# Gathering the heavy group's rows after the first expert's gate product instead of before it

## The reference

```python
def grouped_moe(h, router_w, router_bias, w_gate, w_up, w_down):
    ...
    g = jnp.argmax(group_score, axis=-1)          # each token picks 1 of 4 groups
    ...                                           # and 2 of the 4 experts in it
    for e in range(N_EXPERTS):                    # 16 experts
        a = jax.nn.silu(hf @ w_gate[e]) * (hf @ w_up[e])
        y = y + combine[:, e:e + 1] * (a @ w_down[e])
```

## Time and profile before

| what | value |
|---|---|
| time, median of 3 runs | 2551.22 us (2542.8 to 2553.99) |
| time of the profiled execution | 2548.41 us |
| its span, first to last instruction | 2546.6 us |
| mean granted TensorE clock | 0.987 of full speed |
| busy: TensorE, VectorE, ScalarE | 2426.7, 1694.0, 1304.5 us |
| mean DMA rate over the span | 212 GB/s |
| first mixture (first and last group of instructions looked at) | about 205 to 520 us |
| second mixture | about 755 to 1110 us |

### The profile page before, as it was taken

How to read it: one execution, slowest core, us unless ns; L and a number is a source line. 1 busy time by engine, 2 the same in 40 slices (tenths; PEclk the granted TensorE clock), 3 DMA queues, 4 the chain that set the end, 5 groups by cost and what they waited for, 6 DMA issues and landing times.

```text
span 2546.6 us, 31351 instructions
## 1 busy us (share of the span) xinstructions
PE 2426.7 (95%) x12650; PEld 2057.4 (81%) x12650; DVE 1694.0 (67%) x1521; ACT 1304.5 (51%) x1795; POOL 93.4 (4%) x121
## 2 busy tenths in 40 slices
PE   4989999999899999999999999899997999999999
PEld 3878888887788888879878888788886888987887
DVE  5767988887769787857455565565557655645654
ACT  2555777434547666634445445454455544444443
POOL 1000000111000000000000001000010000000000
PEclk8999999999999999999999999999999999999999
DMA  8815999984519897945535775155551555553553
GB/s 303 289 34 185 368 368 356 358 308 168 217 39 327 301 331 276 365 160 174 195 128 176 190 273 182 61 175 194 193 180 52 184 195 190 174 198 132 177 188 116
DMA packets 229568, 539.80 MB, mean 212 GB/s; under 512 B 20880, under 2 KB 27568, under 8 KB 229424
## 3 DMA queue, kind: packets, MB, share of 16 engines
q1 hardware_dynamic: 207264, 471.82, 53.1%
q0 software_dynamic: 15520, 59.77, 6.4%
q10 hardware_dynamic: 6640, 6.20, 1.3%
HBM read 533.54 MB, written 4.19 MB: 211 GB/s over the span
## 4 chain that ended last, share of the span: by engine, by line
PE 83%; DVE 10%; ACT 3%; issue 2%; DMA 1%; POOL 1%; ACTq 0%; DVEq 0%
PE pair L1041 7%; PE Y L1206 6%; PE Y L1204 6%; PE Y L1215 6%; PE pair L1469 5%; PE pair L1470 5%; PE pair L1475 5%; PE pair L1084 4%; PE pair L1077 4%; PE pair L1078 4%; PE pair L1050 4%; PE Y L1514 3%; PE Y L1516 3%; PE Y L1524 3%; PE pair L1010 2%; PE pair L1019 2%
## 5 line engine op out<-in xcount | busy, mean ns | idle before, releaser
L2316 DVE TENSOR_TENSOR w_low<-raw,w_high 128x2048 fp32r<-128x2048 f32 (+2 forms) x450 | 1016.0, 2273 | 438.8 <-ACT w_high L1858 437.4
L1858 ACT ACTIVATE w_high<-raw 128x1024 fp32r<-128x1024 f32 (+1 forms) x900 | 896.4, 1049 | 554.1 <-PE pair L1470 169.3
L1077 PE MATMUL pair<-w_high,hT 128*128 128x512 f32 (+1 forms) x596 | 233.1, 392 | 1.6 <-ACT work L1913 0.8
L1078 PE MATMUL pair<-w_high,hT 128*128 128x512 f32 (+1 forms) x596 | 231.9, 390 | 0.0
L1206 PE MATMUL Y<-w_high,gated_low 128*128 128x512 f32 x528 | 205.9, 390 | 0.0
L1204 PE MATMUL Y<-w_high,gated_high 128*128 128x512 f32 x528 | 205.9, 390 | 0.0
L1041 PE MATMUL pair<-hT,w_high 128*128 128x512 f32 x768 | 183.0, 390 | 0.5 <-DVE work L2762 0.5
L1041 PEld LDWEIGHTS pair<-hT,w_high 128*128 128x128 f32 x768 | 142.6, 188 | 29.7 <-DVE work L2762 0.9
L1469 PE MATMUL pair<-w_high,rounded 128*128 128x512 f32 x384 | 154.8, 403 | 0.8 <-DVE gated_low L2660 0.8
L1470 PE MATMUL pair<-w_high,rounded 128*128 128x512 f32 x384 | 152.2, 396 | 0.0
L1084 PE MATMUL pair<-w_low,hT 128*128 128x512 f32 (+1 forms) x596 | 146.8, 388 | 4.0 <-DVE w_low L2316 4.0
(11 more groups left out here) (395 smaller groups left out, 3984.3 us busy)
## 6 DMA issues: line engine op xcount, KB each, us to landing
raw<-in_exp_w_gate SPq DMA_DIRECT2D x128, 512.0 KB, 4.6
raw<-in_exp_w_up SPq DMA_DIRECT2D x128, 512.0 KB, 4.8
raw<-in_exp_w_down SPq DMA_DIRECT2D x128, 512.0 KB, 4.6
raw<-in_w_up SPq DMA_DIRECT2D x128, 512.0 KB, 4.6
raw<-in_w_down SPq DMA_DIRECT2D x128, 512.0 KB, 4.3
raw<-in_ret_w_in SPq DMA_DIRECT2D x96, 512.0 KB, 4.7
work<-in_w_mod POOLq DMA_DIRECT2D x40, 1024.0 KB, 8.1
raw<-in_ret_w_out SPq DMA_DIRECT2D x32, 512.0 KB, 4.0
```

The lines of the kernel that those rows point to most:

```text
L1077: nc.tensor.matmul(ps[:, b, 0:n], in_high[:, k0 + kk, bs], high[:, k, :], start=(kk == 0), stop=False)
L1078: last = nc.tensor.matmul(ps[:, b, 0:n], in_low[:, k0 + kk, bs], high[:, k, :], start=False, stop=False)
L1858: nc.scalar.activation(w_high[:, s % HIGH, part], raw[:, s % RAW, part], ACT.Copy).then_inc(high_ready, 1)
L2316: V.tensor_tensor(w_low[:, s % RAW, 0:n], part, w_high[:, s % HIGH, 0:n].bitcast(F32), ALU.subtract).then_inc(low_ready, 1)
```

## The change

The 32 matmuls that gather the heavy windows leave `gather_tokens` for a function of their own, which TensorE calls for the first expert between the second half of the gate product and the first half of the up product. ScalarE's eight heavy copies move from before the first expert's `feed(g + 4)` to behind its `gate_acts`. The instructions, their shapes and their semaphores are the same. VectorE, SyncE and GpSimd have the same programs.

```diff
+            def gather_heavy(m):
+
+                for k in range(KD):
+                    ps, ks = Y[:, k * S:(k + 1) * S], slice(k * P, (k + 1) * P)
+                    for b in range(TB):
+                        nc.tensor.matmul(ps, xn_high[:, b, ks], sel[:, b, SLOTS:], start=(b == 0), stop=False)
+                        last = nc.tensor.matmul(ps, xn_low[:, b, ks], sel[:, b, SLOTS:],
+                                                start=False, stop=(b == TB - 1))
+                last.then_inc(heavy_gathered, 1)
+
             def gather_tokens(m):
...
                     light(j, xn_low, False).then_inc(fill_done, 1)
-                for k in range(KD):
-                    ps, ks = Y[:, k * S:(k + 1) * S], slice(k * P, (k + 1) * P)
-                    for b in range(TB):
-                        nc.tensor.matmul(ps, xn_high[:, b, ks], sel[:, b, SLOTS:], start=(b == 0), stop=False)
-                        last = nc.tensor.matmul(ps, xn_low[:, b, ks], sel[:, b, SLOTS:],
-                                                start=False, stop=(b == TB - 1))
-                last.then_inc(heavy_gathered, 1)
                 use = m.places
...
                     elif at and not follows_heavy:
                         turn(earlier)
+                    if at == 0:
+                        gather_heavy(m)
                     up_free(units)
...
-                se.wait_ge(heavy_gathered, m.nth + 1)
-                for j in range(2):
-                    for i in range(4):
-                        k = 4 * j + i
-                        last = modulated_copy(heavy_tmp[:, j, i, :], Y[:, k * S:(k + 1) * S], k)
-                    last.then_inc(tmp_made, 1)
+
+                def heavy_copies():
+                    se.wait_ge(heavy_gathered, m.nth + 1)
+                    for j in range(2):
+                        for i in range(4):
+                            k = 4 * j + i
+                            last = modulated_copy(heavy_tmp[:, j, i, :], Y[:, k * S:(k + 1) * S], k)
+                        last.then_inc(tmp_made, 1)
...
                     gate_acts(units, g + 1)
+                    if at == 0:
+                        heavy_copies()
```

## The result

| | before | after |
|---|---|---|
| median of 20 runs each | 2551.26 us | 2560.15 us |
| lowest to highest | 2542.8 to 2559.09 | 2550.89 to 2564.38 |
| profiled execution, its span, its clock | 2548.41, 2546.6, 0.987 | 2564.38, 2562.6, 0.984 |

The ratio is 1.0024, with an interval of 1.0013 to 1.0036. So the change costs 0.0024 x 2551 = 6.1 us (3.3 to 9.2), and the kernel is within 0.5% of before, on the slow side. The forecast was +5.7 us. The difference of the two medians, 8.9 us, is larger than the ratio says but inside its interval. I go by the ratio, since it comes with an interval.

A forecast was written before the change was run, and what follows sets the result against it. TensorE, carrying 83% of the chain, was taken to bound the kernel; 2.85 us in the second mixture plus 2.9 in the first gave 5.7 us slower, forecast 2555.5 us, range 2547 to 2562.

The forecast's parts named there:

- the likeliest case: The whole time stays within 0.5% (12.8 us) of the kernel before; chance 0.88, against slower 0.08 and faster 0.04.
- A: Rival, chance 0.08: transfers bound the mixtures and the change is faster, 2.7 us won, 2548.5 us from the median.
- B: Rival, chance 0.12: TensorE's early waits are real, but a later stretch of TensorE absorbs the delay; 2551 us.
- C: Rival, chance 0.15: VectorE's backlog passes in full to TensorE, or the clock falls in both mixtures; 7.8 to 9.5 us.
- Steps 1 and 2: Start of the mixture: TensorE idles 1.4 us before the places, 0.3 before the first gate half, which starts 2.15 early.
- Step 3: Second gate half waits 0.4 us for VectorE's fourth split, starting at 784.8 instead of 786.54, 1.7 us won.
- The working for the first mixture: First mixture with a clock fall of 1.7 us: first down product 2.9 us late; without the fall 1.2 us.
- Steps 5 and 6: Behind the late copies ScalarE's piece 5 starts 3.9 us late; VectorE's 12.0 us to `gated_low` end at 809.4.
- Steps 4 and 7: First up half 2.15 us late, then 0.7 us idle at the first down product: 2.85 us in the second mixture.
- The clock: The granted clock falls to its lower level in the first mixture, 1.7 us lost, and not in the second.

The follow-up runs named there:

- before, again: The kernel before, unchanged, run once more for its profile; from first light gather matmul to first down product 38.21 us (first mixture, clock fell) and 36.69 us (second).
- the filled kernel: The changed kernel with 6 small matmuls put in TensorE's wait before the places; ratio to the kernel before 1.0008 (0.9992 to 1.0024), median 2555.22 us.
- before, more bytes: The kernel before with a 64 KB memory-to-memory DMA added behind each expert piece, 6% more bytes; one run, 2561.06 us.

## Why the prediction was right

The time after, 2560.15 us, is in the range, within 0.5% of before as the likeliest case had it, and the cost of 6.1 us stands beside a forecast of 5.7. The range alone says little, as it holds the times of all three rivals too. The interval of the cost, 3.3 to 9.2 us, rules out A and B but not C. So the forecast stands or falls with its steps.

- *Steps 1 and 2, the places and the first gate half.* Right: 1.07 us idle and some 0.3 us to restart, then 0.17; alone +1.3. From the first light matmul to the first gate matmul, 13.77 us became 11.61, that is 2.16 early, where 2.15 was forecast. In the second mixture it was 12.42, for a reason that the forecast didn't have (below).
- *Step 3, the second gate half.* Right where the clock stayed up: 0.27 us on the matmul and 0.7 on its weight load, and the first up half came 788.00 - 766.36 - 19.46 = 2.18 us late, where 2.15 was forecast (19.46 is 789.34 - 769.88). Where the clock fell, the first half took so long that the split was there in time. This is why a fall costs 1.55 us before and only 0.9 to 1.2 after. The working for the first mixture is wrong here: it puts the 1.7 us of the fall behind the wait for the split, which makes TensorE 2.15 us late at the up half, and it was 1.65 (22.65 us behind the first light matmul against 21.00).
- *Steps 5 and 6.* Right: 3.9 us of waiting for piece 5 on VectorE without a fall, and 12.0 us from there to `gated_low`. With a fall VectorE waits 4.8 to 5.1, and up to 6.1 with a long one.
- *Steps 4 and 7, the sum per mixture.* 0.65 us idle at the down product against 0.7; in all 3.0 us without a fall against 2.85. With a fall in both kernels it is 40.63 to 40.89 less 38.24, or 2.4 to 2.7, against 2.9.
- *The clock.* The forecast took the first mixture with a fall and the second without, as in the one trace it had. The change has it in both, once for 6.9 us behind a late piece. The mean of the four segments of the change is 41.2, of the four of before 37.5: 3.7 us per mixture, 7.5 in all. If the falls came as often in both kernels it would be 5 to 6, from 2.5 to 3.0 per mixture. The measured 6.1 (3.3 to 9.2) holds both, so the size of the clock's part stays open. The mean granted clock of the timed runs doesn't settle it either: 0.9853 over the 20 runs after and 0.9843 to 0.9849 over the runs before, while one more fall in a mixture is worth only 0.0007.

**What the forecast left out.** It gives no price to a piece that lands late. In the second mixture of the change two halves of the second gate piece did, and the first two lines are ScalarE's there. The other two are ScalarE's in the first mixture of "before, again".

```profile
786.52 1.06 ACT L1863 ACTIVATE w_high<-raw 128x1024 fp32r<-128x1024 f32 x1 [0.37 <-DMA raw<-in_exp_w_gate]
...
787.78 1.06 ACT L1863 ACTIVATE w_high<-raw 128x1024 fp32r<-128x1024 f32 x1 [0.21 <-DMA raw<-in_exp_w_gate]
```

```profile
233.51 1.06 ACT L1858 ACTIVATE w_high<-raw 128x1024 fp32r<-128x1024 f32 x1 [0.19 <-DMA raw<-in_exp_w_gate]
234.79 1.06 ACT L1858 ACTIVATE w_high<-raw 128x1024 fp32r<-128x1024 f32 x1 [0.21 <-DMA raw<-in_exp_w_gate]
```

So the late landing doesn't need the change. But in the kernel before the gather covers it: its gate product began 13.75 us behind the first light matmul all the same. After the change ScalarE's copy of the fourth light step, which stands behind that piece, is what TensorE waits for, 0.98 us instead of 0.17, and the gate product began at 12.42. The same happened once more, in the filled kernel's second run (waits of 0.48 and 0.20 us, gate product at 12.50, 42.66 us). These are the only two mixtures with a long fall, so 0.8 to 0.9 us of their 42.6 is a cost of the change that only shows when a piece is late; whether the late piece also made the fall long isn't shown.

**The rivals.** A (the transfers bound it) fell: nothing got faster, and the row of 403 GB/s shows room in the kernel before. The Trainium skill, DMA: Bandwidth & Descriptors, section "Where 436 GB/s comes from", has the HBM side bind at about 358 GB/s; the traces here disagree, with one core working: 366 over an expert and 403 with bytes added. B (absorbed later) fell: in the second mixture the transposes behind the first down product (L1495, L1498) stand at 817.64 before and 831.32 after, 13.68 later, and the last ones at 1117.57 and 1131.22, 13.65 later. In 300 us nothing of the shift was absorbed. C was half right. VectorE's delay isn't passed on in full, as TensorE is late too by then, but its other condition, a fall in both mixtures, held in every profile of the change. The forecast was right at the level of the steps and somewhat lucky in leaving that out.

## What to carry to other kernels

Before independent work is moved away from in front of a consumer, look at what it was hiding: here 3.9 us of gather hid two waits for PSUM buffers, one for a split and now and then a late piece, and moving it made TensorE 2.2 us late out of nothing. Follow each moved step on its second engine as well: ScalarE's queue is in order, so copies that wait for a later gather hold up the weight pieces behind them, and an engine with a backlog (VectorE) passes that on to the next product that needs it. Where runs spread by more than the effect, compare a segment of the trace between two fixed instructions, and sort it by what the clock did.

## What the hardware showed that was not expected

- The segment takes one of a few lengths, mostly by what the clock did: 36.67 to 36.69 or 38.21 to 38.24 before, and 39.7 (filled with six only), 40.6 to 40.9 or 42.6 after. A stretch at the lower level near the first gate product costs 0.9 to 1.6 us when it is some 3.2 to 3.5 us long, and with 6.9 us of it the segment is 2.9 longer, of which 0.8 to 0.9 is the later start of the gate product.
- It isn't the same from run to run: the second mixture of the change had a fall of 6.9 us in one profile and of about 3.4 us in another.
- DMA moved 403 GB/s over 17.1 us ("before, more bytes"), with the share of its engines at 1.05, beside TensorE, VectorE and ScalarE all busy and none of them slower for it.
- A float32 product of 128 columns shows as two matmuls and takes 2.84 / 12 = 0.24 us. A `w_high` product with four times the columns takes the same 0.23 (778.51 - 778.28 in the filled kernel). So a hole of 1.4 us holds six of the small ones, not twelve.
